# Which weight slots lie at column 0 of their ring buffer: slot 1 instead of slot 2, and S_CKV instead of S_UQ

## The reference

```
h = h + 0.5 * swiglu(rmsnorm(h, ffn1_norm[l]), w_gate, w_up, w_down)      # 1024 -> 2816 -> 1024
u = rmsnorm(h, mix_norm[l]);  z = u @ w_in[l]                             # 1024 -> 5536
h = h + merged(latent attention, differential attention, pooling; gates) @ w_out[l]
h = h + 0.5 * swiglu(rmsnorm(h, ffn2_norm[l]), ...)
```

## Time and profile before

| | |
|---|---|
| median of 3 runs | 1472.15 us (1471.96 to 1473.26) |
| profiled execution, its own time | 1472.15 us |
| its span, first to last instruction | 1470.4 us |
| TensorE busy | 1458.3 us, 99% |
| VectorE busy | 1043.6 us, 71% |
| ScalarE busy | 788.5 us, 54% |
| mean granted TensorE clock | 0.997 |

### The profile page before, as it was taken

The page is one execution under the profiler, slowest core; times in us unless marked ns, Lnnn a source line. Parts: engine busy times, 40 slices in busy tenths (PEclk is TensorE's granted clock), DMA queues, the critical chain, the costliest instruction groups (busy, mean ns, idle before and its releaser), DMA issues.

```text
span 1470.4 us, 26788 instructions
## 1 busy us (share of the span) xinstructions
PE 1458.3 (99%) x11602; PEld 1377.7 (94%) x11602; DVE 1043.6 (71%) x1434; ACT 788.5 (54%) x995; POOL 39.4 (3%) x41
## 2 busy tenths in 40 slices
PE   9999999999999999999999999999999999999999
PEld 8999998888999999999999878899999998989978
DVE  6766676786876655766558678777887699676844
ACT  6444455565454444544445566555545645775653
POOL 0000000210000000000001110000000000000000
PEclk9999999999999999999999999999999999999999
DMA  8655545444455555555545444465555453325431
GB/s 322 227 189 189 197 151 201 144 161 154 172 205 186 193 200 198 179 197 201 192 174 184 162 156 149 167 228 206 201 175 199 154 191 133 126 108 194 176 140 58
DMA packets 38405, 262.44 MB, mean 178 GB/s; under 512 B 4624, under 2 KB 5008, under 8 KB 8464
## 3 DMA queue, kind: packets, MB, share of 16 engines
q1 hardware_dynamic: 38144, 260.72, 49.1%
q10 hardware_dynamic: 144, 0.00, 0.0%
HBM read 259.66 MB, written 1.05 MB: 177 GB/s over the span
## 4 chain that ended last, share of the span: by engine, by line
PE 91%; DVE 7%; ACT 1%; issue 1%; DMA 0%; SPq 0%; ACTq 0%
PE ps L243 28%; PE ps L245 28%; PE ps L244 28%; DVE w_low L228 3%; PE ps L1486 1%; DVE scratch L2182 1%; PE ps L1477 0%; PE ps L1459 0%; ACT w_high L222 0%; DMA setup_first<-in_first 0%; PE ps L1501 0%; DVE even_s_rot L2184 0%; PE ps L2764 0%; PE ps L2779 0%; PE ps L2776 0%
## 5 line engine op out<-in xcount | busy, mean ns | idle before, releaser
L228 DVE TENSOR_TENSOR w_low<-w_raw,w_high 128x2048 fp32r<-128x2048 f32 (+2 forms) x244 | 552.0, 2263 | 236.2 <-ACT w_high L222 236.1
L222 ACT ACTIVATE w_high<-w_raw 128x2048 fp32r<-128x2048 f32 (+2 forms) x244 | 462.0, 1895 | 448.7 <-PE ps L245 444.6
L243 PE MATMUL ps<-x,w_high 128*128 128x256 f32 x1864 | 520.4, 279 | 2.7 <-DVE w_low L897 1.9
L245 PE MATMUL ps<-x,w_low 128*128 128x256 f32 x1864 | 516.2, 277 | 0.0
L244 PE MATMUL ps<-x,w_high 128*128 128x256 f32 x1864 | 516.1, 277 | 0.0
L243 PEld LDWEIGHTS ps<-x,w_high 128*128 128x128 f32 x1864 | 350.3, 188 | 5.8 <-DVE x L839 2.1
L244 PEld LDWEIGHTS ps<-x,w_high 128*128 128x128 f32 x1864 | 350.3, 188 | 0.8 <-issue 0.5
L245 PEld LDWEIGHTS ps<-x,w_low 128*128 128x128 f32 x1864 | 350.3, 188 | 0.0
L243 PE MATMUL ps<-w_high,x 128*128 128x512 f32 (+1 forms) x448 | 165.9, 370 | 0.0
L245 PE MATMUL ps<-w_high,x 128*128 128x512 f32 (+1 forms) x448 | 161.2, 360 | 0.0
L244 PE MATMUL ps<-w_low,x 128*128 128x512 f32 (+1 forms) x448 | 161.0, 359 | 0.0
(11 more groups left out here) (469 smaller groups left out, 2016.3 us busy)
## 6 DMA issues: line engine op xcount, KB each, us to landing
w_raw<-in_weights SPq DMA_DIRECT2D x231, 1024.0 KB, 4.8
w_raw<-in_weights SPq DMA_DIRECT2D x10, 768.0 KB, 4.3
w_raw<-in_weights SPq DMA_DIRECT2D x5, 512.0 KB, 4.2
even_second_vectors<-in_second SPq DMA_DIRECT2D x1, 1836.0 KB, 8.6
setup_first<-in_first SPq DMA_DIRECT2D x3, 512.0 KB, 5.9
resid<-in_x SPq DMA_DIRECT2D x1, 1024.0 KB, 10.8
out<-resid SPq DMA_DIRECT2D x3, 256.0 KB, 2.5
table<-in_table SPq DMA_DIRECT2D x1, 737.0 KB, 8.8
```

The costliest lines, as they stand in the source:

```text
L222: act.activation(self.slot(self.wh, n), self.slot(self.raw, n), ACT.Copy).then_inc(self.hi_made, 1)
L228: dve.tensor_tensor(self.slot(self.wl, n), self.slot(self.raw, n), self.slot(self.wh, n).bitcast(F32), ALU.subtract).then_inc(self.lo_made, 1)
L243: pe.matmul(out, ah, bh, start=start, stop=False, skip_group_check=True)
L245: return pe.matmul(out, al, bh, start=False, stop=stop, skip_group_check=True)
```

## The change

The entry at column 0 moves. In the mixers it is slot 1 (S_CKV) instead of slot 4 (S_UQ); S_OUT stays. In all FFNs but the first it is slot 1 instead of slot 2; the table slots of the last FFN stay. The first FFN, the even layer and the odd layer are unchanged. A slot that is no longer an entry goes to column 24.

```
-MIX_ENTRIES, EVEN_ENTRIES = (S_UQ, S_OUT), (A_GLU,)
+MIX_ENTRIES, EVEN_ENTRIES = (S_CKV, S_OUT), (A_GLU,)
...
-FIRST_AT, APART_AT, LAST_AT = ffn_at((2,)), ffn_at((2,)), ffn_at((2, *TABLE_SLOTS))
+FIRST_AT, APART_AT, LAST_AT = ffn_at((2,)), ffn_at((1,)), ffn_at((1, *TABLE_SLOTS))
```

## The result

The changed kernel takes 1488.26 us (median of 4 runs, 1486.4 to 1492.77) against 1472.06 us before: a ratio of 1.0117, with a 95% interval of 1.009 to 1.0145. It is 16 us slower. The forecast of 1472.2 us and its range were wrong; the first of its rivals, priced at 1490.0 us, is what happened.

A forecast was written before the change was run, and what follows sets the result against it. TensorE was taken to bound the kernel, busy 1458.3 of 1470.4 us. FFNs -0.33, layer 0 mixer +0.09 and layer 1 mixer +0.32 summed to +0.08 us, so 1472.2 us; range for 8 in 10: 1470.2 to 1474.4.

The forecast's parts named there:

- the first of its rivals: FFNs: slot 1 at column 0 doesn't end the slow pace; 85 slots cost 18.3 us, 1490.0 us; chance 0.10 (one stage or more).
- the border behind slot 1: Three FFNs, column 0 to 24: slow pace ends, slots 2 and 3 take 5.44 us; -0.11 us a stage, -0.33 together.
- its 12 borders: Places in the earlier trace where a slot at column 0 gives way to another; 10 ended the slow pace.
- the late stretch: Second table slot to slot 5 of the even layer: rival that it turns quick, 2.6 us, 1469.6 us; chance 0.06.
- The halves of slot 1: Three FFNs: first half 2.79 us, about 2.80 with the gap (+0.08); half behind the mean 3.00 (-0.01).
- Mixer 0: Layer 0 mixer: L1561 waits for VectorE, slot 3 stays slow at 6.05 us, S_UQ 4.24, S_UKV +0.05; sum +0.09 us.
- Mixer 1: Layer 1 mixer: L1561 starts 0.04 us late behind a wait, slot 3 turns slow (+0.18), S_UQ and S_UKV +0.05 each; +0.32.
- The order at L1561: Layer 1 mixer: TensorE, last before, would arrive at 783.74, ahead of VectorE's result, so the load starts at 783.82.
- the forecast's own other outcome: Layer 1 mixer: if slot 3 stays quick, S_UQ gains 0.11 us and the mixer's sum is -0.07 us.
- The two SBUF ports: TensorE: skill's rule that weights and streamed operand use separate ports, so columns' places make no difference; sum 0, chance 0.04.

The follow-up runs named there:

- e9: FFN part of the change alone, mixers as before, with every norm's mean made by four fp32 matmuls instead of one; 1476.52 us.
- e5: FFN part of the change alone, mixers as before, with the mean of the three FFNs three products later in slot 1 (21 left); 1473.54 us.
- e6: FFN part of the change alone, mixers as before, with 30 products before the mean in slot 1 and 18 behind it; 1471.72 us.
- e8: The kernel before, unchanged, profiled a second time; 1473.21 us.
- e2: Mixer part of the change alone, FFNs keeping slot 2 at column 0 as in the kernel before; 1471.63 us, ratio 0.9995.
- e14: Kernel before, with entries at slot 3 in the first FFN and slots 24, 27, 30 in the last; 1468.68 us, ratio 0.9986.
- e4: Kernel before, with no slot at column 0 in the three FFNs but the table slots; 1479.16 us.
- e1: FFN part of the change alone, mixers as in the kernel before; 1489.08 us, ratio 1.0111.

## Why the prediction was wrong

- **The failed step** is the border behind slot 1: "slot 2 goes from 5.61 to 5.44, -0.17, and slot 3 from 5.45 to 5.44", in three stages. They took 5.65 and 5.65, and so did every slot behind them up to the next thing that ends the pace: 29 more slots in two of the stages, 19 in the last FFN. The support was "the first FFN has the same line, the same `mean` in the same middle of a slot of the same shape". The slot's shape was the same; the mean wasn't: four fp32 matmuls at L402 against one at L357. e9 shows that this difference alone turns the border of the three FFNs quick, e5 and e6 that with one matmul a shift of the border by 3 or 6 products does. Nor is the first FFN itself reliable: over 14 profiles its border was quick in 12 and slow in 2.
- **The evidence lay in the trace of before.** 2 of its 12 borders were slow, and I counted them instead of asking what set them apart. One of them, behind slot 29 of the last FFN, ends "117 120 | 116", the very pattern of the changed kernel.
- **The rival was right**, in place and in size: 17.85 us against 17.8 at slot 23, and 1490.0 against a measured 1488.26. It had a chance of 0.10. That 1490.0 lies so near the median is in part luck: the profiled execution got back 1.65 us in the late stretch and 2.9 us by the clock.
- **The halves of slot 1** were right: 2.80 and 3.00 us.
- **Mixer 0**: L1561 waits for VectorE as forecast, its load at 208.29, 0.06 behind the end of L1318. Slot 3 took 6.06, S_UQ 4.24, S_UKV +0.07. That slot 3 was slow again was luck (e8, e2). Not foreseen: S_DK stayed slow too, +0.19. By slot 8 the mixer had lost 0.28 us, where the sum had +0.09.
- **Mixer 1**: wrong by 0.4 us, -0.07 from slot 1 to slot 8 instead of +0.32. The order at L1561 didn't turn round:

```profile
796.74 0.69 DVE L1318 TENSOR_TENSOR mix_arena<-table,mix_inv_sum 128x512 f32<-128x512 f32 x1
```

```profile
797.40 0.19 PEld L245 LDWEIGHTS ps<-x,w_low 128*128 128x128 f32 x1
797.52 0.30 PEld L1561 LDWEIGHTS ps<-mix_arena,ones 128*128 128x128 f32 x2
```

  The load stands 0.12 behind the one before it, its usual distance, and 0.09 behind L1318's end at 797.43. The first half of S_DQ wasn't quick (the same failed border), so TensorE didn't gain the 0.11 that was to bring it there first. Slot 3 stayed quick at 5.87 and S_UQ gained 0.11. That is the forecast's own other outcome, -0.07, reached for another reason.
- **A small misreading**: the row of 5.47 us for slot 0 in the earlier trace rows opens 0.03 us ahead of the slot's first matmul, at 405.00; the slot took 5.44. Nothing hangs on it.
- **The two SBUF ports.** The sum by that rule was 0. The Trainium skill (TensorE: Matmul & The Clock Gate, "Part 2: What happens when you issue a matmul") has the weights and the streamed operand on ports of their own. The runs don't show whether the ports are independent. They show that the same 48 products take 5.44 to 5.66 us by the columns and by what ran before, so the 0 doesn't hold.
- **Open**: why the gaps run in these cycles, what in the machine has a period of four products, and what the 120 place does. The place at the border forecasts the pace in all 191 cases; what it is a sign of isn't shown.

## What to carry to other kernels

When two cases in a trace behave differently at what looks like the same place, find what separates them before giving chances by their count. A pace that survives from one stage to the next is priced by how far it runs (here 85 slots), not by the place at which it is decided. And an edit that rests on a delicate state should be put where the state is always entered in the same way: the slot behind the mean rather than the one that holds it. In e14 the borders bear that out, all 12 of them quick; a gain in time isn't shown.

## What the runs showed of the hardware that I had not expected

- A matmul pace can last: with the same instructions at the same columns, 48 products of 256 columns take 5.44 us or 5.65 us, and it stays so over 31 slots (175 us) until something else comes between.
- A single fp32 matmul in a slot at column 24 flipped the pace in e4: quick in and slow out, or slow in and quick out (gaps of 118 118 117 ns against 113 113 114).
- Where in a cycle of four products the weights' column changes goes with the pace that follows: 25 of 25 slow in one place, 110 of 110 quick in two others. Moving the mean by 3 or 6 products was worth 15.5 and 17.4 us (e5 and e6 against e1).
- Some executions of a kernel are some 6.6 us longer than others (15 of 82 of the kernel before), and in the three profiles at that level the first stage was in the slow pace. Another 3 us or so come and go with the clock, which is granted at half for 6.8 us in the even layer in some executions and not in others.
